# A chain of thirteen transformer stages on one core: first stage from x laid out by feature, gate rows ahead of a tile's turn, other banks in the forgetting attention

## The chip, the cores and the metric

The kernel runs on one core of a Trainium2 chip. The metric is the device time of one execution in microseconds; a lower one is better. Times are medians over several executions on the same chip. The core has a matrix engine (TensorE, PE in the profile), a vector engine (VectorE, DVE), an activation engine (ScalarE, ACT), a general engine (GpSimd, POOL) and a queue engine (SyncE, SP). Each runs its own list of instructions in order; semaphores hold one engine until another has come to a point.

## The reference

There are 256 tokens of 1024 features in float32. Two layers and a third block follow each other. Cut to what matters:

```python
x = x + 0.5 * swiglu(rmsnorm(x, g), w_in, w_out)        # stage 0, and four more like it
x = x + hgrn2_mixer(rmsnorm(x, g), ...)                 # layer 0
x = x + fox_mixer(rmsnorm(x, g), ...)                   # layer 1: forgetting attention, 16 heads of 64
h = h + 0.5 * gate * rms_norm(swiglu_2(u, ...), post)   # u = rms_norm(h, pre) * (1 + scale) + shift
h = h + gate * rms_norm(token_mixer(u, ...), post)      # third block: shift, scale and gate come from c
h = h + 0.5 * gate * rms_norm(swiglu_2(u, ...), post)

def rmsnorm(x, g): return x * rsqrt(mean(x * x) + 1e-6) * g
def swiglu(h, w_in, w_out): gate, up = split(h @ w_in); return (silu(gate) * up) @ w_out   # width 2816
```

## The kernel before

Every product is done in three parts: an operand is split into a rounded half (`w_hi`, `actT_hi`) and the rest (`w_lo`, `actT_lo`), and TensorE adds hi x hi, hi x lo and lo x hi into one bank of PSUM. SyncE's queue loads weights into four slots of `raw` (a slot is 128 x 2048 numbers, four blocks of 128 features by 512 columns), ScalarE rounds a slot into `w_hi` (L1370), VectorE subtracts (L1928). The activations come as features by tokens: TensorE transposes the scaled rows `xn` (L611, `turn_tile`), ScalarE rounds them out of PSUM with the norm's weight as scale (L1389) and VectorE makes the rest (L1950).

A feed-forward stage works through 11 chunks of 256 hidden columns (512 with the gate's). The gate and up products of a chunk fill bank 4 (tile 0) and bank 5 (tile 1), each tile of 128 tokens takes 24 products. ScalarE applies silu to the gate's half of a bank, first tile 0 (L1519, waits for `up0_done`), then tile 1 (L1523), and VectorE multiplies by the up half (L2095). Only then may `up(c + 1, 0)` write the same bank. In chunks 1 to 10 the down products of the chunk before lie in between; between chunk 0 and chunk 1 there is nothing.

The first chunk of a stage is `rounded_first`: tile 0's 16 products with `actT_hi` (L654), then its 8 with `actT_lo` (L662) with `between()` in their middle, then tile 1's. `between()` transposes tile 1, and in the third block's feed-forward stages (norm 6 and norm 8) also writes a row of gates across the partitions with 8 transposes (L835, `gate_wide_row`), which nothing needs until the stage's end.

The stage at the start: SyncE loads tile 0 of x, eight quarter-slot pieces of weights (256 KB each; slot 0, then slot 1), tile 1 of x, and two pieces of slot 3. ScalarE's queue loads the identity matrix and the norm's weights as rows. TensorE runs five products of ones to start (L1332), turns the weights' rows into columns, then tile 0. Later vectors (72 columns of biases among them) are loaded as rows by eleven DMAs of GpSimd and turned by two transposes after chunk 4 (`turn_vectors`, L1342 and L1343).

In the forgetting attention TensorE writes the negative running sum of the log gates into bank 5 (L1007), VectorE copies and splits it (L2343 to L2350), and the turned queries and keys of the first half go to banks 6, 7, 4, 5 (L1019), those of the second half to banks 1, 2, 3, 7. Keys are copied out of the first two banks by VectorE (L2356), queries out of the last two by ScalarE (L1687). Products of later column units, `unit(c, t)`, go to bank 0 for tile 0 and to bank 7 for tile 1.

## Time and profile before

| | us |
|---|---|
| median of 3 runs (lowest, highest) | 1580.67 (1580.09, 1581.17) |
| the profiled execution's own time | 1580.04 |
| its span in the trace | 1578.2 |
| TensorE busy | 1563.0 |
| VectorE busy | 1130.0 |
| ScalarE busy | 825.0 |

The trace covers one execution. The span runs from the first to the last instruction; 1.84 us of the profiled time lie around it. A row of the timeline is one instruction or several alike (x4), with its start and duration in us; brackets at its end tell how long its engine had been idle and what ended that.

### The profile page before, as it was taken

How to read it: one execution, taken by the hardware profiler on the slowest of the kernel's cores; microseconds unless marked ns; L12 is line 12 of the kernel's file. 1: busy time of each engine (PE TensorE's matmuls, PEld its weight loads, DVE VectorE, ACT ScalarE, POOL GpSimd, SP SyncE). 2: the span in 40 equal slices, each digit the busy share in tenths (PEclk: the TensorE clock that was granted, in tenths of full speed). 3: DMA queues.
4: the chain of work that ended last, by engine and by line, in shares of the span. 5: the costliest groups of instructions: out<-in, count | busy, mean ns of one | idle time of the engine just before them, and what ended most of it. 6: DMA issues, size and time to landing. Idle time of an engine off the chain costs nothing.

```text
span 1578.2 us, 22308 instructions
## 1 busy us (share of the span) xinstructions
PE 1563.0 (99%) x8273; PEld 1294.6 (82%) x8273; DVE 1130.0 (72%) x1271; ACT 825.0 (52%) x1007; POOL 67.1 (4%) x101
## 2 busy tenths in 40 slices
PE   8999999999999999999999999999999999999998
PEld 6888888888888888887888888888887988878886
DVE  6565668868776877776867877787787567775654
ACT  6465564654445544465655444554447666574443
POOL 2000100000000000000000000000000000000000
PEclk9999999999999999999999999999999999999999
DMA  8766653359887688845345988668884444456662
GB/s 281 223 206 215 228 200 123 129 173 299 278 264 260 209 276 281 280 165 182 109 159 186 301 265 276 236 217 271 274 306 153 171 161 149 145 173 214 210 208 87
DMA packets 242385, 337.09 MB, mean 214 GB/s; under 512 B 14217, under 2 KB 180322, under 8 KB 242320
## 3 DMA queue, kind: packets, MB, share of 16 engines
q1 hardware_dynamic: 196320, 281.05, 53.9%
q0 software_dynamic: 11232, 39.33, 6.8%
q10 hardware_dynamic: 34768, 15.83, 4.0%
q8 instruction: 42, 0.69, 0.2%
q14 instruction: 23, 0.19, 0.0%
HBM read 319.38 MB, written 1.05 MB: 203 GB/s over the span
## 4 chain that ended last, share of the span: by engine, by line
PE 94%; DVE 3%; ACT 2%; DMA 1%; issue 0%; SPq 0%; DVEq 0%; ACTq 0%
PE ps L602 28%; PE ps L604 28%; PE ps L603 28%; PE ps L654 3%; PE ps L662 2%; PE ps L611 1%; DVE w_lo L1928 1%; ACT w_hi L1370 1%; DMA raw<-ffn_w_in_dram 1%; DVE arena L1963 0%; PE ps L877 0%; PE ps L1037 0%; PE ps L1063 0%; PE ps L1187 0%; ACT arena L1418 0%
## 5 line engine op out<-in xcount | busy, mean ns | idle before, releaser
L1928 DVE TENSOR_TENSOR w_lo<-raw,w_hi 128x2048 fp32r<-128x2048 f32 x264 | 601.7, 2288 | 198.0 <-ACT w_hi L1370 196.9
L1370 ACT CAST w_hi<-raw 128x2048 fp32r<-128x2048 f32 x264 | 502.1, 1911 | 322.1 <-PE ps L604 290.1
L602 PE MATMUL ps<-w_hi,actT_hi 128*128 128x512 f32 x1392 | 546.5, 393 | 1.1 <-ACT arena L1687 0.7
L604 PE MATMUL ps<-w_hi,actT_lo 128*128 128x512 f32 x1392 | 542.1, 389 | 0.0
L603 PE MATMUL ps<-w_lo,actT_hi 128*128 128x512 f32 x1392 | 541.8, 389 | 0.0
L602 PEld LDWEIGHTS ps<-w_hi,actT_hi 128*128 128x128 f32 x1392 | 261.3, 188 | 57.9 <-issue 3.3
L604 PEld LDWEIGHTS ps<-w_hi,actT_lo 128*128 128x128 f32 x1392 | 261.3, 188 | 54.6
L603 PEld LDWEIGHTS ps<-w_lo,actT_hi 128*128 128x128 f32 x1392 | 261.4, 188 | 53.3
L602 PE MATMUL ps<-w_hi,hT_hi 128*128 128x512 f32 x480 | 187.4, 390 | 0.0
L604 PE MATMUL ps<-w_hi,hT_lo 128*128 128x512 f32 x480 | 186.9, 389 | 0.0
L603 PE MATMUL ps<-w_lo,hT_hi 128*128 128x512 f32 x480 | 186.8, 389 | 0.0
L2095 DVE TENSOR_TENSOR hidden<-gate,ps 128x256 f32<-128x256 f32 x132 | 77.9, 595 | 84.8 <-ACT gate L1523 76.2
L602 PEld LDWEIGHTS ps<-w_hi,hT_hi 128*128 128x128 f32 x480 | 90.1, 188 | 18.8
L603 PEld LDWEIGHTS ps<-w_lo,hT_hi 128*128 128x128 f32 x480 | 90.1, 188 | 18.7
L604 PEld LDWEIGHTS ps<-w_hi,hT_lo 128*128 128x128 f32 x480 | 90.1, 188 | 18.7
L1523 ACT ACTIVATE gate<-ps 128x256 f32<-128x256 f32 x66 | 25.4, 384 | 143.8 <-PE ps L604 124.1
L2113 DVE SCALAR_TENSOR_TENSOR arena<-arena,c_silu 128x512 f32<-128x512 f32 x126 | 94.3, 748 | 2.5
L593 POOL DMA_DIRECT2D arena<-w_ada_dram x72 | 51.3, 712 | 924.2 <-DVE arena L2113 634.2
L654 PE MATMUL ps<-w_hi,actT_hi 128*128 128x512 f32 x144 | 57.3, 398 | 3.5 <-ACT actT_hi L1389 2.9
L654 PE MATMUL ps<-w_lo,actT_hi 128*128 128x512 f32 x144 | 56.2, 391 | 0.0
L1519 ACT ACTIVATE gate<-ps 128x256 f32<-128x256 f32 x66 | 25.3, 384 | 54.3 <-PE ps L604 54.2
L2080 DVE STREAM_TRANSPOSE arena<-hidden 128x512 f32<-128x512 f32 x60 | 42.7, 712 | 3.8
(304 smaller groups left out, 1301.3 us busy)
## 6 DMA issues: line engine op xcount, KB each, us to landing
raw<-ffn_w_in_dram SPq DMA_DIRECT2D x172, 512.0 KB, 4.9
raw<-ffn_w_out_dram SPq DMA_DIRECT2D x88, 512.0 KB, 4.6
arena<-w_ada_dram POOLq DMA_DIRECT2D x72, 512.0 KB, 5.3
raw<-ffn_w_gate_dram SPq DMA_DIRECT2D x44, 512.0 KB, 4.0
raw<-ffn_w_up_dram SPq DMA_DIRECT2D x44, 512.0 KB, 5.0
raw<-ffn_w_down_dram SPq DMA_DIRECT2D x44, 512.0 KB, 4.4
raw<-w_in_dram SPq DMA_DIRECT2D x40, 512.0 KB, 4.5
raw<-hg_w_in_dram SPq DMA_DIRECT2D x32, 512.0 KB, 4.7
```

Of the source, the lines that this page charges most:

```text
L593: nc.gpsimd.dma_start(ada_raw[:, n % 2, :, :], w_ada[:, ks:ks + ADA_KS, j * ADA_FOLD:(j + 1) * ADA_FOLD])\
L602: nc.tensor.matmul(to, hi, whi, start=start, stop=False, skip_group_check=True)
L603: nc.tensor.matmul(to, hi, wlo, start=False, stop=False, skip_group_check=True)
L604: return nc.tensor.matmul(to, lo, whi, start=False, stop=stop, skip_group_check=True)
L654: nc.tensor.matmul(to, actT_hi[:, k, tok], half[:, s, w], start=k == 0 and half is w_hi, stop=False, skip_group_check=True)
L662: last = nc.tensor.matmul(to, actT_lo[:, k, tok], w_hi[:, s, w], start=False, stop=k == KD - 1, skip_group_check=True)
L1370: nc.scalar.copy(w_hi[:, s, :], raw[:, s, :]).then_inc(hi_ready[s], 1)
L1523: nc.scalar.activation(gate[:, 1, :], ps[:, UP_BANK + 1, 0:FC], ACT.Silu).then_inc(gate_ready, 1)
L1928: nc.vector.tensor_tensor(w_lo[:, s, :], raw[:, s, :], w_hi[:, s, :].bitcast(F32), ALU.subtract)\
L2080: nc.vector.transpose(hid_blocks.rearrange("p b n -> p (b n)"), hidden.rearrange("p t f -> p (t f)"))\
L2095: nc.vector.tensor_tensor(to, g, u, ALU.mult).then_inc(hidden_ready, 1)
L2113: total = nc.vector.scalar_tensor_tensor(acc_j, part, c_silu[:, k:k + 1], acc_j, ALU.mult, ALU.add)
```

## The change

It has four parts.

1. Stage 0 reads a second copy of x that is already features by tokens (`x_turned`, prepared with the other inputs). ScalarE rounds it with the norm's weight as scale, VectorE makes the rest, without the token's factor 1/rms. GpSimd squares x and adds the eight feature blocks into one, TensorE sums over the partitions with two products of one column, and the factor is applied behind the products: as the scale of the silu and as a factor in the product with the up half. TensorE no longer transposes anything in stage 0. Its first chunk is `loaded_chunk`, in which both tiles go side by side, in parts of four products, in the order in which the halves of the slots and their rests come. x itself is loaded later, for the residual.
2. All small vectors come as one table of columns (`columns`), so `turn_vectors` and eleven loads fall away.
3. In `between()` the row of gates comes ahead of tile 1's transposes.
4. In the forgetting attention the running sum goes to bank 3 in place of bank 5, and VectorE's copy of it is waited for within `chunk(1, 1)`, ahead of its second tile; the second half's keys and queries go to banks 7, 1, 2, 3.

```diff
+                        if half == 0:
+                            nc.sync.dma_start(x_turned[:, 4:8, :], a["x_turned"][:, 4:8, :]).then_inc(x_turned_loaded, 16)
...
-            load_x(0)
+                nc.sync.dma_start(x[:, t, :], a["x"][0, t * P:(t + 1) * P, :]).then_inc(x_loaded, 16)
...
                     up_weights(st, 2)
+                    if st.norm == 0:
+                        load_x(0)
+                        load_x(1)
...
+            pool.wait_ge(head_loaded, 32)
+            step.mark(nc.gpsimd.tensor_tensor(x_squares[:, 0:4, :], x_turned[:, 0:4, :], x_turned[:, 0:4, :], ALU.mult))
+            pool.wait_ge(x_turned_loaded, 16)
+            step(nc.gpsimd.tensor_tensor(x_squares[:, 4:8, :], x_turned[:, 4:8, :], x_turned[:, 4:8, :], ALU.mult))
+            for n in (4, 2):
+                step(nc.gpsimd.tensor_tensor(x_squares[:, 0:n, :], x_squares[:, 0:n, :], x_squares[:, n:2 * n, :], ALU.add))
+            nc.gpsimd.tensor_tensor(x_squares[:, 0, :], x_squares[:, 0, :], x_squares[:, 1, :], ALU.add).then_inc(squares, 2)
             pool.wait_ge(actT_ready, 4)
-            at = 48
...
             nc.gpsimd.dma_start(fox_b, a["fox_b_f"]).then_inc(small_loaded, 16)
...
-            nc.gpsimd.dma_start(consts[:, P:], a["consts"][:, P:]).then_inc(consts_loaded, 16)
+            nc.gpsimd.dma_start(consts[:, :], a["consts"]).then_inc(consts_loaded, 16)
...
                 def between():
-                    turn_tile(st, xn, 1)
                     if st.kind == "ffn" and st.norm >= 6:
                         gate_wide_row(st.norm - 6)
+                    turn_tile(st, xn, 1)
                 rounded_first(st, banks[0], 0, between).then_inc(tile0_done, 1)
                 rounded_first(st, banks[1], 1)
...
+            def loaded_chunk(st):
+                def part(s, kks, act, weights, start=False, stop=False):
+                    for t in range(TILES):
+                        for kk in kks:
+                            k, w = 4 * s + kk, slice(kk * COLS, (kk + 1) * COLS)
+                            last = nc.tensor.matmul(ps[:, UP_BANK + t, :], act[:, k, t * P:(t + 1) * P], weights[:, s, w],
+                                                    start=start and kk == 0, stop=stop and kk == 3, skip_group_check=True)
+                        if stop and t == 0:
+                            last.then_inc(up0_done, 1)
+                    return last
...
+                def sums():
+                    pe.wait_ge(squares, 2)
+                    for t in range(TILES):
+                        last = nc.tensor.matmul(ps[:, SMALL_BANK, t:t + 1], x_squares[:, 0, t * P:(t + 1) * P], hidden[:, 0, 0:1],
+                                                start=True, stop=True, skip_group_check=True)
+                    last.then_inc(first_sum, 1)
+                for s in range(2):
+                    pe.wait_ge(actT_hi_ready, s + 1)
+                    pe.wait_ge(front_hi, s + 1)
+                    part(s, (0, 1), actT_hi, w_hi, start=s == 0)
+                    if s == 0:
+                        pe.wait_ge(front_lo, 1)
+                        part(s, (0, 1), actT_hi, w_lo)
+                    pe.wait_ge(actT_ready, s + 1)
+                    part(s, (0, 1), actT_lo, w_hi)
+                    if s:
+                        pe.wait_ge(front_lo, 2)
+                        part(s, (0, 1), actT_hi, w_lo)
+                        sums()
+                    pe.wait_ge(hi_ready[s], 1)
+                    part(s, (2, 3), actT_hi, w_hi)
+                    part(s, (2, 3), actT_lo, w_hi)
+                    pe.wait_ge(lo_ready[s], 1)
+                    part(s, (2, 3), actT_hi, w_lo, stop=s == 1).then_inc(split_used[s], 1)
...
-                first_chunk(st, [ps[:, UP_BANK + t, :] for t in range(TILES)], up0_done)
+                if st.norm:
+                    first_chunk(st, [ps[:, UP_BANK + t, :] for t in range(TILES)], up0_done)
+                else:
+                    loaded_chunk(st)
...
+                with pe.Fori(2, NF - 1) as c:
+                    middle(c)
                 if st.norm == 0:
-                    with pe.Fori(2, VECTORS_AT) as c:
-                        middle(c)
-                    turn_vectors()
-                    with pe.Fori(VECTORS_AT, NF - 1) as c:
-                        middle(c)
-                else:
-                    with pe.Fori(2, NF - 1) as c:
-                        middle(c)
+                    pe.wait_ge(consts_loaded, 32)
...
+                        if t and s % 2 == 0 and second_tile is not None:
+                            second_tile()
...
-                    nc.tensor.matmul(ps[:, 5, 0:T], C["neg_spread"][0:FOX_H, :], fx_cT, start=True, stop=True)                        .then_inc(fx_spread, 1)
+                    pe.wait_ge(kept1, st.kept + 2)
+                    nc.tensor.matmul(ps[:, 3, 0:T], C["neg_spread"][0:FOX_H, :], fx_cT, start=True, stop=True)                        .then_inc(fx_spread, 1)
...
-                        if bank == 5:
-                            pe.wait_ge(fx_negc_ready, 3)
...
-                chunk(st, 1, 1)
+                chunk(st, 1, 1, lambda: pe.wait_ge(fx_negc_ready, 3))
...
-                turn(1, (1, 2, 3, 7))
+                turn(1, (7, 1, 2, 3))
                 weigh(0)
-                pe.wait_ge(fx_qT_ready, 4)
+                pe.wait_ge(fx_kT_ready, 3)
...
-            pe.wait_ge(head_loaded, 32)
-            nc.tensor.transpose(ps[:, SMALL_BANK, 0:48], rows_a[0:48, :], ident[0:48, 0:48]).then_inc(cols_turned, 1)
-            warm(1)
...
-                if st.norm == 0:
-                    turn_tile(st, xn, 0)
...
+            def first_stage(st):
+                def front(s):
+                    act.wait_ge(front_loaded[s], 32)
+                    nc.scalar.copy(w_hi[:, s, 0:SLOT // 2], raw[:, s, 0:SLOT // 2]).then_inc(front_hi, 1)
+                def back(s):
+                    act.wait_ge(raw_loaded[s], 32)
+                    nc.scalar.copy(w_hi[:, s, SLOT // 2:SLOT], raw[:, s, SLOT // 2:SLOT]).then_inc(hi_ready[s], 1)
+                def rounded(s):
+                    for k in range(4 * s, 4 * s + 4):
+                        last = nc.scalar.activation(actT_hi[:, k, :], x_turned[:, k, :], ACT.Copy, scale=norm_cols[:, k:k + 1])
+                    last.then_inc(actT_hi_ready, 3 if s else 1)
+                front(0)
+                act.wait_ge(head_loaded, 32)
+                rounded(0)
+                back(0)
+                act.wait_ge(x_turned_loaded, 16)
+                rounded(1)
+                front(1)
+                back(1)
+                split_hi(3, st.filled[3])
+                act.wait_ge(first_sum, 1)
+                nc.scalar.activation(n_std[:, 0:2], ps[:, SMALL_BANK, 0:2], ACT.Sqrt, bias=eps_col, scale=1.0 / D).then_inc(stds, 2)
...
+                    scale = [first_rstd[:, t:t + 1] if st.norm == 0 else 1.0 for t in range(TILES)]
+                    if st.norm == 0:
+                        act.wait_ge(first_scale, 1)
                     act.wait_ge(up0_done, n + c + 1)
-                    nc.scalar.activation(gate[:, 0, :], ps[:, UP_BANK, 0:FC], ACT.Silu).then_inc(gate_ready, 1)
+                    nc.scalar.activation(gate[:, 0, :], ps[:, UP_BANK, 0:FC], ACT.Silu, scale=scale[0]).then_inc(gate_ready, 1)
...
-                queries(1, (3, 7))
+                queries(1, (2, 3))
...
-            nc.scalar.dma_start(ident, a["consts"][:, 0:P]).then_inc(head_loaded, 16)
-            nc.scalar.dma_start(rows_a[0:48, :], a["norm_g"].rearrange("l i (k p) -> (l i k) p", p=P)).then_inc(head_loaded, 16)
+            nc.scalar.dma_start(x_turned[:, 0:4, :], a["x_turned"][:, 0:4, :]).then_inc(head_loaded, 16)
+            nc.scalar.dma_start(cols[:, 0:COLUMNS], a["columns"]).then_inc(head_loaded, 16)
             act.wait_ge(memsets_done, 2)
             load_sqrt()
-            after_out(None, stages[0])
+            first_stage(stages[0])
...
+            def first_stage(st):
+                def rest(s, part):
+                    at = slice(part * SLOT // 2, (part + 1) * SLOT // 2)
+                    if part:
...
+                        dve.wait_ge(front_hi, s + 1)
                     nc.vector.tensor_tensor(w_lo[:, s, at], raw[:, s, at], w_hi[:, s, at].bitcast(F32), ALU.subtract)\
-                        .then_inc(lo, 1)
+                        .then_inc(lo_ready[s] if part else front_lo, 1)
...
+                def unrounded(s):
+                    dve.wait_ge(actT_hi_ready, s + 1)
+                    for k in range(4 * s, 4 * s + 4):
+                        last = nc.vector.scalar_tensor_tensor(actT_lo[:, k, :], x_turned[:, k, :], norm_cols[:, k:k + 1],
+                                                              actT_hi[:, k, :].bitcast(F32), ALU.mult, ALU.subtract)
+                    last.then_inc(actT_ready, 3 if s else 1)
+                rest(0, 0)
+                dve.wait_ge(head_loaded, 32)
+                unrounded(0)
+                rest(0, 1)
+                dve.wait_ge(x_turned_loaded, 16)
+                unrounded(1)
+                rest(1, 0)
+                rest(1, 1)
+                split_lo(3, st.filled[3])
+                dve.wait_ge(stds, 2)
+                nc.vector.reciprocal(first_rstd, n_std[:, 0:2]).then_inc(first_scale, 1)
...
+                    if st.norm == 0 and t == 0:
+                        dve.wait_ge(x_loaded, 32)
...
@@ -2092,7 +2151,10 @@
                         to, g, u = hidden[:, t, :], gate[:, t, :], ps[:, UP_BANK + t, FC:COLS]
                         if turn:
                             to, g, u = hidden_block(t), by_block(g), by_block(u)
-                        nc.vector.tensor_tensor(to, g, u, ALU.mult).then_inc(hidden_ready, 1)
+                        if st.norm == 0:
+                            nc.vector.scalar_tensor_tensor(to, u, first_rstd[:, t:t + 1], g, ALU.mult, ALU.mult).then_inc(hidden_ready, 1)
+                        else:
+                            nc.vector.tensor_tensor(to, g, u, ALU.mult).then_inc(hidden_ready, 1)
...
-                keys(1, (1, 2))
+                keys(1, (7, 1))
...
-    arrays = {name: np.ascontiguousarray(inputs[name]) for name in INPUTS}
+    arrays = {name: np.ascontiguousarray(inputs[name]) for name in INPUTS if name not in COLUMN_INPUTS}
+    arrays["columns"] = columns(inputs)
+    arrays["x_turned"] = np.ascontiguousarray(np.asarray(inputs["x"])[0].T.reshape(KD, P, T).transpose(1, 0, 2))
```

How the instructions stand, at the three places that the prediction speaks of. First ScalarE at the program's start; before, from the rounding of slot 3 to the first silu (`gate` is the silu's output, `ps` is PSUM):

```order
L1370 CAST w_hi<-raw 128x2048 [waits raw_loaded3]
L1389 ACTIVATE actT_hi<-ps,cols 128x128 [waits turned]
L1389 ACTIVATE actT_hi<-ps,cols 128x128 x3
L1389 ACTIVATE actT_hi<-ps,cols 128x128 [waits turned]
L1389 ACTIVATE actT_hi<-ps,cols 128x128 x3
L1519 ACT_TABLE_LOAD
L1519 ACTIVATE gate<-ps 128x256 [waits up0_done]
L1523 ACTIVATE gate<-ps 128x256 [waits split_used1]
```

And with the change, from the first rounding of x on:

```order
L1493 ACTIVATE actT_hi<-arena,cols 128x256 [waits head_loaded]
L1493 ACTIVATE actT_hi<-arena,cols 128x256 x3
L1489 CAST w_hi<-raw 128x1024 [waits raw_loaded0]
L1493 ACTIVATE actT_hi<-arena,cols 128x256 [waits x_turned_loaded]
L1493 ACTIVATE actT_hi<-arena,cols 128x256 x3
L1485 CAST w_hi<-raw 128x1024 [waits front_loaded1]
L1489 CAST w_hi<-raw 128x1024 [waits raw_loaded1]
L1387 CAST w_hi<-raw 128x2048 [waits raw_loaded3]
L1506 ACTIVATE small<-ps,small 128x2 [waits first_sum]
L1553 ACT_TABLE_LOAD [waits up0_done]
L1553 ACTIVATE gate<-ps,small 128x256 [waits first_scale]
L1557 ACTIVATE gate<-ps,small 128x256 [waits split_used1]
```

The table load stood ahead of any wait and now stands behind the wait for `up0_done`; the silu itself waits for `first_scale`. Next TensorE at the end of the first chunk (`arena` holds the squares, `hidden` the ones). Before, the last rows of tile 1 and the first of chunk 1:

```order
L654 MATMUL ps<-w_lo,actT_hi 128x512
L654 MATMUL ps<-w_hi,actT_hi 128x512
L654 MATMUL ps<-w_lo,actT_hi 128x512
L662 MATMUL ps<-w_hi,actT_lo 128x512 [waits actT_ready]
L662 MATMUL ps<-w_hi,actT_lo 128x512 x3
L662 MATMUL ps<-w_hi,actT_lo 128x512 [waits actT_ready]
L662 MATMUL ps<-w_hi,actT_lo 128x512 x3
L602 MATMUL ps<-w_hi,actT_hi 128x512 [waits hidden_ready,lo_ready3]
L603 MATMUL ps<-w_lo,actT_hi 128x512
L604 MATMUL ps<-w_hi,actT_lo 128x512
```

With the change:

```order
L675 MATMUL ps<-w_hi,actT_lo 128x512 [waits actT_ready]
L675 MATMUL ps<-w_hi,actT_lo 128x512 x3
L675 MATMUL ps<-w_lo,actT_hi 128x512 [waits front_lo]
L675 MATMUL ps<-w_lo,actT_hi 128x512 x3
L684 MATMUL ps<-hidden,arena 128x1 [waits squares]
L684 MATMUL ps<-hidden,arena 128x1
L675 MATMUL ps<-w_hi,actT_hi 128x512 [waits hi_ready1]
L675 MATMUL ps<-w_hi,actT_hi 128x512 x3
L675 MATMUL ps<-w_hi,actT_lo 128x512 x4
L675 MATMUL ps<-w_lo,actT_hi 128x512 [waits lo_ready1]
L675 MATMUL ps<-w_lo,actT_hi 128x512 x3
L598 MATMUL ps<-w_hi,actT_hi 128x512 [waits hidden_ready,lo_ready3]
```

Tile 0's last product stood 25 products ahead of chunk 1; now it stands among the last four. Last, TensorE in the forgetting attention, before, from the running sum to the next chunk of weights:

```order
L1007 MATMUL ps<-arena,consts_sb 128x256 [waits fx_c]
L1019 MATMUL ps<-consts_sb,arena 128x128 [waits fx_normed]
L1019 MATMUL ps<-consts_sb,arena 128x128 x11
L1019 MATMUL ps<-consts_sb,arena 128x128 [waits fx_negc_ready]
L1019 MATMUL ps<-consts_sb,arena 128x128 x3
L602 MATMUL ps<-w_hi,actT_hi 128x512 [waits lo_ready2,kept1,kept0]
L603 MATMUL ps<-w_lo,actT_hi 128x512
```

With the change:

```order
L1037 MATMUL ps<-arena,consts_sb 128x256 [waits kept1,fx_c]
L1047 MATMUL ps<-consts_sb,arena 128x128 [waits fx_normed]
L1047 MATMUL ps<-consts_sb,arena 128x128 x15
L598 MATMUL ps<-w_hi,actT_hi 128x512 [waits lo_ready2,kept1,kept0]
L599 MATMUL ps<-w_lo,actT_hi 128x512
```

The wait for the split running sum (`fx_negc_ready`) is gone from between the transposes; it now stands twelve products further on.

## Rows read from the trace of the kernel before

**Rows 1.** The page's first lines: span, and busy time of each engine.

```profile
span 1578.2 us, 22308 instructions
...
PE 1563.0 (99%) x8273; PEld 1294.6 (82%) x8273; DVE 1130.0 (72%) x1271; ACT 825.0 (52%) x1007; POOL 67.1 (4%) x101
```

**Rows 2.** Waits of TensorE over the span: us in total, times, longest.

```profile
PE ps L654 <- ACT actT_hi L1389: 2.9, 3, 1.9
```

**Rows 3.** Timeline, 5 to 16 us: start, us, engine, line, operation, [idle before].

```profile
5.86 0.70 PE L1332 MATMUL ps<-hidden 128*128 128x256 f32 x2
...
6.49 1.05 ACT L1470 CAST w_hi<-raw 128x1024 fp32r<-128x1024 f32 x1
...
7.57 1.23 DVE L1935 TENSOR_TENSOR w_lo<-raw,w_hi 128x1024 fp32r<-128x1024 f32 x1
8.00 1.04 ACT L1472 CAST w_hi<-raw 128x1024 fp32r<-128x1024 f32 x1 [0.47 <-DMA raw<-ffn_w_in_dram]
8.95 1.14 ACT L1389 ACTIVATE actT_hi<-ps,cols 128x128 fp32r<-128x128 f32 x4
...
10.14 0.50 PE L654 MATMUL ps<-w_hi,actT_hi 128*128 128x512 f32 x1 [1.86 <-ACT actT_hi L1389]
10.22 1.12 DVE L1950 SCALAR_TENSOR_TENSOR actT_lo<-ps,cols,actT_hi 128x128 fp32r<-128x128 f32 x4
...
15.20 1.91 ACT L1370 CAST w_hi<-raw 128x2048 fp32r<-128x2048 f32 x1 [0.76 <-DMA raw<-ffn_w_in_dram]
```

**Rows 4.** Timeline, 19 to 25 us: the first activations and products behind chunk 0.

```profile
19.20 1.28 ACT L1519 ACT_TABLE_LOAD   x1
...
20.49 0.39 ACT L1519 ACTIVATE gate<-ps 128x256 f32<-128x256 f32 x1
...
23.77 0.39 PE L602 MATMUL ps<-w_hi,actT_hi 128*128 128x512 f32 x1
...
23.97 0.38 ACT L1523 ACTIVATE gate<-ps 128x256 f32<-128x256 f32 x1 [3.09 <-PE ps L662]
...
24.00 0.39 PE L603 MATMUL ps<-w_lo,actT_hi 128*128 128x512 f32 x1
...
24.39 0.62 DVE L2095 TENSOR_TENSOR hidden<-gate,ps 128x256 f32<-128x256 f32 x1 [2.37 <-ACT gate L1523]
```

**Rows 5.** GpSimd's groups of instructions: busy us, mean ns, idle before.

```profile
L580 POOL CAST hidden<-arena 128x112 uint8<-128x112 f32 x1 | 2.4, 2396 | 153.4 <-PE ps L711 153.4
L582 POOL MEMSET arena<- 128x2048 f32 x1 | 1.8, 1811 | 0.1
```

**Rows 6.** Windows of TensorE at the end: busy us (count), granted clock, DMA.

```profile
1574.00:1578.20 4.20, 0.00 (x0) 0.72 0.33 125
```

**Rows 7.** Timeline of TensorE at 89 us, around the turned vectors.

```profile
88.83 0.39 PE L604 MATMUL ps<-w_hi,hT_lo 128*128 128x512 f32 x1
89.06 0.26 PE L1342 MATMUL ps<-consts_sb,arena 116*128 116x116 f32 x1
...
89.50 0.40 PE L603 MATMUL ps<-w_lo,actT_hi 128*128 128x512 f32 x1
```

**Rows 8.** Timeline in the forgetting attention, at 734 us.

```profile
733.90 0.66 PE L1019 MATMUL ps<-consts_sb,arena 128*128 128x128 f32 x4 [0.47 <-DVE hT_lo L2350]
```

**Rows 9.** Timeline in the forgetting attention, at 771 us.

```profile
771.42 0.50 PE L602 MATMUL ps<-w_hi,actT_hi 128*128 128x512 f32 x1 [0.74 <-ACT arena L1687]
```

**Rows 10.** Timeline of the last feed-forward stage's start.

```profile
1394.42 1.09 PE L611 MATMUL ps<-consts_sb,arena 128*128 128x128 f32 x8 [1.22 <-DVE arena L1974]
...
1395.36 1.04 PE L835 MATMUL ps<-consts_sb,mod_gate 128*128 128x128 f32 x8
...
1399.69 1.36 DVE L1963 TENSOR_SCALAR arena<-ps,mod_scale,modc 128x128 f32<-128x128 f32 x4
...
1401.08 0.69 DVE L1966 TENSOR_TENSOR actT_lo<-arena,actT_hi 128x512 fp32r<-128x512 f32 x1
```

**Rows 11.** Timeline of the stage before the mixer, at 1032 us.

```profile
1031.72 0.50 PE L662 MATMUL ps<-w_hi,actT_lo 128*128 128x512 f32 x1 [0.50 <-DVE actT_lo L1966]
```

97 lines of the change are left out of this document (31 added, 66 removed).

## Prediction

> **What bounds the kernel now.** I read the page's first lines first: TensorE is busy for 1563.0 of the span's 1578.2 us [rows 1], so only about 15 us are not already its own work, and whatever the other engines save is worth nothing unless TensorE waited for it. So next come TensorE's waits: the largest group is 2.9 us in three waits for the rounding of x (L1389) at the start, the longest 1.9 [rows 2]. Then I read the timeline at each place that the change touches. At the start TensorE gets its first real product at 10.14 us, after 1.86 idle [rows 3], and the first product of chunk 1 at 23.77 [rows 4]. Products follow each other every 0.23 us (23.77 to 24.00 [rows 4]), although a row shows 0.39 for one, because they overlap. In the forgetting attention there are two waits, 0.47 us for the split running sum [rows 8] and 0.74 us for ScalarE's copy of the queries [rows 9]. In the third block TensorE waits 1.22 us ahead of tile 1's transposes [rows 10] and 0.50 us at the end of another first chunk [rows 11].
>
> **Part 1, the start.** Two times decide: when the first product can start and when chunk 1 can start.
>
> Loads: slot 0 had landed at 8.00 and slot 3 at 15.20 (both casts waited for their DMA [rows 3]). Between them 2.5 MB came, so 2.88 us per MB. Ahead of 8.00 stood x's tile (0.5 MB), some 0.09 MB of small things and slot 0 (1 MB). Now `x_turned`'s first half, the columns and slot 0 stand there, the same sum. So slot 0's front half is there 0.5 MB earlier, at 6.5, `x_turned`'s second half at 8.0 + 1.4 = 9.4, slot 1 by 12.3 and slot 3 as before at 15.2.
>
> ScalarE: the front half takes 1.05 [rows 3], 6.5 to 7.55. Then four roundings of 128x256: four of 128x128 took 1.14; the slope of the casts (1.91 for 2048 columns, 1.05 for 1024 [rows 3]) adds 0.11 to each, so 1.6, to 9.15. First product at 9.2 in place of 10.14. Further: back half to 10.2, second roundings to 11.8, slot 1 to 13.9, slot 3 from 15.2 to 17.1, all of it early (below).
>
> VectorE: 1.23 for the front's rest (7.6 to 8.8), then four rests of x: 1.12 for 128x128 [rows 3], and about 0.13 more each, 1.65, so 9.2 to 10.85. TensorE wants them after eight products, at 11.0. I name this cover because it is the thinnest: 0.15 us. The later halves end at 12.1, 13.75, 15.0 and 16.2, and TensorE wants them after 20, 28, 32 and 44 products, at 13.8, 15.6, 16.6 and 19.6.
>
> So TensorE runs 48 products without a gap, 11.0 us, and two products of one column, for which I take 0.3 (two transposes cost 0.2, below): 9.2 to 20.5. That is 3.3 us ahead of 23.77. Most of it is not kept. Chunk 1 writes the same bank and waits for tile 0's hidden values. Before, tile 0 was complete 25 products earlier, and ScalarE loaded silu's table at 19.20 and was through at 20.9 [rows 4], long ahead of TensorE. Now tile 0's last product starts 0.7 ahead of the end and is complete at about 20.2. And the order of instructions shows the table load behind the wait for `up0_done`. So from 20.2: 1.28 table load, 0.39 silu, 0.62 product of VectorE [rows 4], and 0.1 for three hand-overs (VectorE started 0.04 behind its silu): 22.6. Gain of part 1: 23.77 - 22.6 = 1.1 us, with a new idle stretch of TensorE of about 2.1 us. What is queued behind it is all of TensorE's work; VectorE's hidden value of tile 1 follows in 0.6, ahead of tile 0's twelve products.
>
> Of the table load the row shows 1.28 and the silu 0.01 behind it [rows 4]. The Trainium skill (ScalarE: Activation LUTs, What ACT_TABLE_LOAD costs) adds a drain of about 1.38 to each switch of sets; by that the new idle stretch would be 3.5 and the kernel 1579.5. The row does not show such a drain, so I leave it out.
>
> The same move of the load is in the loop that runs after the small vectors, five passes. There tile 1's silu waits for twelve more products, 2.8 us, and 1.28 + 0.39 lie within these. Cost nothing; without that cover up to 5 x 1.28 = 6.4 us.
>
> Squares: GpSimd has four of its five operations, 2816 columns, behind the landing at 9.4. No row shows such an operation. A memset of 2048 columns takes 1.81 [rows 5]: 2.5 us for 2816, done at 11.9. A cast of 112 columns takes 2.40 [rows 5]: if that is a fixed price of an instruction, 4 x 2.4 + 2.5 = 12.1, done at 21.5. TensorE asks after 36 products, at 17.5. A product of two inputs moves about three times what a memset does, which gives 7.4 us and 16.8; I take that, no wait, and keep 4.0 us as the upper end. The skill (GPSIMD Engine Reference, Elementwise — side-by-side cycle accounting) has 4.5 us for 2048 columns of an addition; that would be done at 15.6, and the sum stays.
>
> Vectors: `turn_vectors` stretched 88.83 to 89.50 by 0.67 where two products take 0.46 [rows 7]: gain 0.2. The eleven loads that fall away ran beside the products. x's two loads move behind chunk 2's weights; the residual wants them at the stage's end, some 170 us on. Slot 1's second filling is asked for when VectorE is done with the first, 16.2; 1 MB at 2.88 and some 2 us on the way land near 21.5, and ScalarE turns to it at 22. It is wanted after chunk 1's first half, 5.5 us later than 22.6, so a late landing has 1 to 2 us of cover.
>
> **Part 3, gate rows first.** The eight transposes take 0.9 us (1394.42 to 1395.36 for their like) and would fit into the wait of 1.22 [rows 10]. But the chunk's end is VectorE's: its last block starts at 1399.69, takes 1.36, and the rest another 0.69 from 1401.08 [rows 10], done at 1401.8. TensorE arrived there at 1395.36 + 0.9 + 24 x 0.23 = 1401.8 before. So arriving 0.6 to 0.9 earlier only makes a wait there: gain 0. In the other stage the transposes of tile 1 come 0.9 later, ScalarE's rounding with them, and the wait of 0.50 for VectorE at 1031.72 [rows 11] takes that up: cost 0. Together I keep +0.9 and -0.4 as ends.
>
> **Part 4, banks.** The wait of 0.47 [rows 8] goes: `fx_negc_ready` is now wanted twelve products (2.8 us) later and came at 733.9. TensorE's new wait on bank 3 is for a copy that `chunk(1, 1)` waited for anyway. The wait of 0.74 [rows 9] goes too: bank 7 is turned first and read by VectorE, which is idle there, and ScalarE's copies come behind its exponentials as before, but nobody waits for them. Gain 0.5 + 0.7 = 1.2. No TensorE row shows a wait between there and the end of that stage that it could reappear in. Ends: 0.6 and 1.2.
>
> **Sum.** 1.1 + 0.2 + 0 + 1.2 = 2.5 us. Against the profiled execution's 1580.04 that is 1577.5; the median of the runs is 0.6 above that execution, so 1578.2. A measurement of this kernel can tell about 0.2% (3.2 us) from no change; 2.5 us is 0.16%.
>
> **Rivals.**
> - *More comes back*: the load of the table is not paid behind `up0_done`, the head lands earlier than 6.5, or gate rows pay 0.9. With 1.3 for the first: 3.8 us, 1576.9. For it: my times at the start use bounds that were waits on other things. Against: the order of the instructions is plain.
> - *Squares late*: GpSimd needs more than 8.1 us from 9.4. Up to the fixed price it is 4.0 us lost, 1582.2; from 13.8 us on (5.7 lost) the kernel is slower by more than 0.2%. Nothing else covers it, since TensorE's last twelve products stand behind the two small ones.
> - *Slower by the clock*: the products of ones end near 6.6 [rows 3] and TensorE then idles 2.6 us in place of 1.86. In the last 4.2 us of the trace, where TensorE does nothing, the granted clock is 0.72 [rows 6], so it does fall from 2.4 to 1.2 GHz in idleness. At the lower level a product takes 0.23 us more; 25 such products (5.7 us) make it slower by over 0.2%, all 48 give 1578.2 + 11 = 1589. Against: the waits of 1.86 and less did not let it fall.
> - *The start does nothing*: `x_turned` lands 1.4 us late on the shared queues and part 1 is worth 0: 1579.3.
>
> **Chances.** Forecast 0.55 (1577.3 to 1579.0, of which 0.05 falls under 1577.5), more 0.22, squares late 0.14 (0.10 within 0.2%, 0.04 beyond), clock 0.04, start does nothing 0.05. So faster 0.27, same 0.65, slower 0.08. The range reaches down to 1576.4 (the forecast with table load and gate rows less a little) and up to 1580.9 (a wait of 2.7 us for the squares).
>
> **What would show it.** Right: first product near 9.2; a table load of ScalarE right behind tile 0's last product; chunk 1 from about 22.6; no wait at the two places of the forgetting attention; a longer wait for VectorE's rest at the end of the last stage's first chunk. Wrong: a wait of TensorE for GpSimd ahead of the one-column products, a granted clock under 1 in the first 20 us, products spaced over 0.23, or a TensorE wait in the last stage that is gone without another in its place.

## The result and the profile after

The changed kernel takes 1587.68 us (median of 6 runs, 1585.78 to 1588.15), the kernel before 1580.92 in the same comparison. The ratio is 1.0043 with a 95% interval of 1.0031 to 1.0054: 6.8 us slower. The forecast was 1578.2 (1576.4 to 1580.9), and slower by over 0.2% had a chance of 0.08.

The profiled execution took 1587.27 us with a span of 1585.5, so 7.3 more than before's 1578.2 [rows 1]. The page's first lines:

```profile
span 1585.5 us, 22260 instructions
...
PE 1566.1 (99%) x8258; PEld 1296.7 (82%) x8258; DVE 1133.1 (71%) x1255; ACT 822.3 (52%) x994; POOL 68.6 (4%) x95
```

TensorE is busy 3.1 us longer, although it has 15 products fewer: a first hint that some ran slower. The rest is waiting. Its three longest waits (us in total, times, longest), all of the first stage:

```profile
PE ps L675 <- DVE actT_lo L1979: 3.7, 1, 3.7
PE ps L675 <- ACT actT_hi L1493: 3.2, 1, 3.2
PE ps L598 <- DVE hidden L2155: 2.2, 1, 2.2
```

The third was forecast (2.1), the second nearly (2.6). The first, on VectorE's `actT_lo` of L1979, the rests of x, was not. The timeline around it (start, us, then the idle time ahead in brackets), to be held against [rows 3]:

```profile
7.08 1.04 ACT L1485 CAST w_hi<-raw 128x1024 fp32r<-128x1024 f32 x1 [3.82 <-DMA raw<-ffn_w_in_dram]
...
8.16 1.75 DVE L1973 TENSOR_TENSOR w_lo<-raw,w_hi 128x1024 fp32r<-128x1024 f32 x1 [8.16 <-ACT w_hi L1485]
...
9.79 1.62 PE L675 MATMUL ps<-w_hi,actT_hi 128*128 128x512 f32 x4 [3.19 <-ACT actT_hi L1493]
...
9.85 6.90 DVE L1979 SCALAR_TENSOR_TENSOR actT_lo<-arena,cols,actT_hi 128x256 fp32r<-128x256 f32 x4
...
16.81 1.77 PE L675 MATMUL ps<-w_hi,actT_lo 128*128 128x512 f32 x4 [3.69 <-DVE actT_lo L1979]
17.81 1.66 DVE L1979 SCALAR_TENSOR_TENSOR actT_lo<-arena,cols,actT_hi 128x256 fp32r<-128x256 f32 x4
```

The first cast starts at 7.08, when its DMA has landed (6.5 in the forecast), and the first product at 9.79, 0.35 ahead of before's 10.14. Behind its eighth product TensorE waits 3.69 us, because four rests of x take 6.90 us. The same four instructions on the other half of x, from 17.81, take 1.66. The only difference that the trace shows is what GpSimd does meanwhile. In narrow stretches of the timeline of GpSimd and then of VectorE the instructions of that stretch stand one by one:

```profile
9.80 1.89 POOL L561 TENSOR_TENSOR arena<-arena 128x1024 f32<-128x1024 f32 x1 [0.97 <-DMA arena<-x_turned_dram]
...
11.77 2.43 POOL L563 TENSOR_TENSOR arena<-arena 128x1024 f32<-128x1024 f32 x1
...
14.27 1.33 POOL L563 TENSOR_TENSOR arena<-arena 128x512 f32<-128x512 f32 x1
...
15.75 0.72 POOL L564 TENSOR_TENSOR arena<-arena 128x256 f32<-128x256 f32 x1
...
9.85 2.12 DVE L1979 SCALAR_TENSOR_TENSOR actT_lo<-arena,cols,actT_hi 128x256 fp32r<-128x256 f32 x1
...
11.89 2.59 DVE L1979 SCALAR_TENSOR_TENSOR actT_lo<-arena,cols,actT_hi 128x256 fp32r<-128x256 f32 x1
...
14.40 1.48 DVE L1979 SCALAR_TENSOR_TENSOR actT_lo<-arena,cols,actT_hi 128x256 fp32r<-128x256 f32 x1
...
15.81 0.95 DVE L1979 SCALAR_TENSOR_TENSOR actT_lo<-arena,cols,actT_hi 128x256 fp32r<-128x256 f32 x1
```

Add start and duration. GpSimd's operations end at 11.69, 14.20, 15.60 and 16.47; VectorE's rests end at 11.97, 14.48, 15.88 and 16.76. Each rest ends 0.28 or 0.29 us behind one operation of GpSimd: VectorE gets one instruction through for each of GpSimd's, however long that is. The row at 8.16 fits in: a rest of weights takes 1.75 there (1.23 before [rows 3]) beside GpSimd's first square, which runs from 6.94 to 8.83.

The second loss is the clock. TensorE's windows (from and to, us, busy, count, granted clock as a share of full speed, then DMA's share and GB/s):

```profile
10.00:15.00 5.00, 3.12 (x8) 0.66 0.99 312
15.00:20.00 5.00, 3.19 (x8) 0.72 0.00 1
...
25.00:30.00 5.00, 3.29 (x17) 1.00 1.04 369
30.00:35.00 5.00, 4.46 (x13) 0.66 1.05 348
```

Before, the same windows all show 1.00. Now the granted clock fell from 2.4 to 1.2 GHz just behind the idle stretch of 3.19 us, just behind the one of 3.69, and again just behind the 2.25 ahead of chunk 1 (narrower windows show it at half from about 10.4, 17.2 and 30.8). Behind that last one nine products take from 30.54 to 34.25, 3.71 us in place of 2.07.

How chunk 1 comes to start at 30.54 (before 23.77 [rows 4]):

```profile
27.92 1.28 ACT L1553 ACT_TABLE_LOAD   x1 [2.15 <-PE ps L675]
29.22 0.47 ACT L1553 ACTIVATE gate<-ps,small 128x256 f32<-128x256 f32 x1
...
30.54 0.50 PE L598 MATMUL ps<-w_hi,actT_hi 128*128 128x512 f32 x1 [2.25 <-DVE hidden L2155]
```

The table load stands behind `up0_done`, as forecast, and the silu follows it at once.

The other parts went nearly as forecast. Neither wait of [rows 8, 9] has a like in the changed kernel. New is an idle stretch of 0.59 us of TensorE at 266.51, in layer 0, for which the trace shows no cause ("issue"). In the last stage, to be held against [rows 10]:

```profile
1401.68 1.10 PE L607 MATMUL ps<-consts_sb,arena 128*128 128x128 f32 x8 [0.35 <-DVE arena L2031]
...
1408.35 0.69 DVE L2023 TENSOR_TENSOR actT_lo<-arena,actT_hi 128x512 fp32r<-128x512 f32 x1
```

The wait ahead of tile 1's transposes is 0.35 in place of 1.22, and VectorE's last rest stands where it stood: from 1408.35, 7.27 behind before's 1401.08 [rows 10]. The stage's first product is as late, 1395.76 against 1388.51, so the stage gained nothing.

### The profile page after: what moved, and what is told of

The parts are those of the page before. It is cut to its first block, busy times and chain, and to the rows that moved or that the text cites. A ratio compares the mean times of both kernels' runs of the same rounds, so it can differ in the third digit from the quotient of the medians.

```text
span 1585.5 us, 22260 instructions
## 1 busy us (share of the span) xinstructions
PE 1566.1 (99%) x8258; PEld 1296.7 (82%) x8258; DVE 1133.1 (71%) x1255; ACT 822.3 (52%) x994; POOL 68.6 (4%) x95
## 3 DMA queue, kind: packets, MB, share of 16 engines
HBM read 320.43 MB, written 1.05 MB: 203 GB/s over the span
## 4 chain that ended last, share of the span: by engine, by line
PE 94%; DVE 3%; ACT 1%; issue 1%; DMA 0%; DVEq 0%; SPq 0%; ACTq 0%
PE ps L598 28%; PE ps L600 28%; PE ps L599 28%; PE ps L645 3%; PE ps L653 1%; PE ps L607 1%; DVE w_lo L1962 1%; PE ps L675 1%; DVE arena L2020 1%; PE ps L906 0%; PE ps L1065 0%; PE ps L1108 0%; DMA raw<-ffn_w_in_dram 0%; PE ps L1091 0%; PE ps L1215 0%
## 5 line engine op out<-in xcount | busy, mean ns | idle before, releaser
L2157 DVE TENSOR_TENSOR hidden<-gate,ps 128x256 f32<-128x256 f32 x110 | 64.1, 591 | 65.3 <-ACT gate L1557 58.0
L1557 ACT ACTIVATE gate<-ps 128x256 f32<-128x256 f32 x55 | 21.1, 384 | 115.3 <-PE ps L600 99.6
L1545 ACT CAST hT_hi<-arena 128x512 fp32r<-128x512 f32 x60 | 36.9, 616 | 27.7 <-DMA arena<-arena 27.7
L2144 DVE TENSOR_TENSOR hT_lo<-arena,hT_hi 128x512 fp32r<-128x512 f32 x60 | 41.1, 686 | 9.6 <-ACT hT_hi L1545 9.6
```

The lines of the kernel that those rows point to most:

```text
L1545: nc.scalar.copy(hT_hi.rearrange("p f t -> p (f t)").rearrange("p (n a j) -> p n a j", n=4, a=4), hT_columns)\
L1557: nc.scalar.activation(gate[:, 1, :], ps[:, UP_BANK + 1, 0:FC], ACT.Silu, scale=scale[1]).then_inc(gate_ready, 1)
L2144: nc.vector.tensor_tensor(hT_lo.rearrange("p f t -> p (f t)").rearrange("p (n a j) -> p n a j", n=4, a=4), hT_columns, hT_hi.bitcast(F32). ...
L2157: nc.vector.tensor_tensor(to, g, u, ALU.mult).then_inc(hidden_ready, 1)
```

## The experiments

The main theory is that GpSimd's squares hold VectorE's rests of x, and that the waits of TensorE that this makes also pull its clock down. Each expectation names its rivals. "Ratio" is always to the kernel before, with its 95% interval.

**The changed kernel without GpSimd's operations.** The factor 1/rms is made from ones, so this version leaves out the norm's scale.

```diff
-            step.mark(nc.gpsimd.tensor_tensor(x_squares[:, 0:4, :], x_turned[:, 0:4, :], x_turned[:, 0:4, :], ALU.mult))
...
+            nc.gpsimd.memset(small[:, 24:25], 0.0).then_inc(squares, 2)
```

> The changed kernel without GpSimd's five operations: the factor 1/rms is made from ones in place of the squares of x, so stage 0 is not scaled rightly. Theory A (GpSimd's two-input operations hold VectorE up): VectorE's four rests of x from 9.9 us take 1.7 us in place of 6.90, TensorE's wait of 3.7 us behind its eighth product is gone, and with it the second stretch at the lower clock; the first stretch stays, since TensorE still idles 3.2 us ahead of its first product. Time 1581.5 to 1583. Rival B (the rests are slow because of their own form, two inputs from SBUF and a column as scalar, or because they are the first of their kind): 6.9 us stays and the time stays at 1587.

1581.76 us, ratio 1.0007 (0.9998 to 1.0016): 5.7 us of the 6.8 lost are gone (0.0036 of 1581). Its timeline:

```profile
10.08 2.07 PE L669 MATMUL ps<-w_hi,actT_hi 128*128 128x512 f32 x4 [4.21 <-ACT actT_hi L1487]
10.15 1.67 DVE L1973 SCALAR_TENSOR_TENSOR actT_lo<-arena,cols,actT_hi 128x256 fp32r<-128x256 f32 x4 [0.47 <-ACT actT_hi L1487]
...
26.39 0.47 PE L592 MATMUL ps<-w_hi,actT_hi 128*128 128x512 f32 x1 [2.25 <-DVE hidden L2149]
```

Four rests take 1.67 us and no wait for them is left. The clock was still low here from about 8.4 to 15.2 (it fell in the 4.21 us of idle ahead of the first product), so the low clock at the start alone is not what cost most. The profile is the slowest of this version's ten runs (1583.34 us), with an idle stretch like that of layer 0 above, here 1.1 us.

**The same operations put into the kernel before**: six products of two inputs on a spare region, nothing else changed.

```diff
+            for n in (1024, 1024, 1024, 1024, 512, 256):
+                step(nc.gpsimd.tensor_tensor(spare[0][:, 0:n], spare[0][:, 0:n], spare[1][:, 0:n], ALU.mult))
```

> The kernel before with six two-input operations of GpSimd from 5.4 us on (4 x 1024, 512 and 256 columns of a spare region that nothing reads), about 9 us of them. Theory A (GpSimd holds VectorE up): VectorE's subtractions of 1024 columns take 1.7 us or more in place of 1.23 while GpSimd works, its scaling of x and rests of x too, TensorE's first product comes 1 to 4 us later, 1583 to 1588. Rival B: VectorE's durations stay and the time is 1580.9.

1587.47 us, ratio 1.0043 (1.0028 to 1.0059). Nobody waits for these results, and yet they cost 6.8 us. GpSimd's and then VectorE's timeline:

```profile
5.31 14.53 POOL L562 TENSOR_TENSOR arena<-arena 128x1024 f32<-128x1024 f32 x6 [2.45 <-DMA arena<-norm_g_dram]
...
6.49 3.95 DVE L1981 TENSOR_SCALAR arena<-x,small 128x512 f32<-128x512 f32 x2
10.35 6.68 DVE L1942 TENSOR_TENSOR w_lo<-raw,w_hi 128x1024 fp32r<-128x1024 f32 x2
16.96 1.11 DVE L1957 SCALAR_TENSOR_TENSOR actT_lo<-ps,cols,actT_hi 128x128 fp32r<-128x128 f32 x4
```

The like in VectorE's timeline of before:

```profile
6.65 0.88 DVE L1974 TENSOR_SCALAR arena<-x,small 128x512 f32<-128x512 f32 x2
...
11.26 2.35 DVE L1935 TENSOR_TENSOR w_lo<-raw,w_hi 128x1024 fp32r<-128x1024 f32 x2
```

The operation with one input in SBUF (TENSOR_SCALAR) takes 3.95 in place of 0.88; two weights' rests with both inputs in SBUF take 6.68 in place of 2.35; four rests with one input in PSUM take 1.11, as before (1.12 [rows 3]), while GpSimd still runs. So it is not GpSimd's activity as such but access to SBUF. The 6.8 us are again hold and clock together: the granted clock is at half from about 10 to 23.6.

**Only writes in that place**: eight memsets of GpSimd in the kernel before.

```diff
+            for n in range(8):
+                step(nc.gpsimd.memset(spare, 1.0))
```

> The kernel before with eight memsets of GpSimd over 128x2048 of a spare region (1.81 us each by its own row, about 14.6 us, from 5.3 to 20), where the earlier run had six two-input operations in the same stretch. They only write. Theory A (what holds VectorE is GpSimd's reading of two inputs beside VectorE's second input): the weights' rests stay at 1.23 each and the four-fold rests at 1.12, and the time is 1581 within 0.15%; at most the operation with one input in SBUF (the TENSOR_SCALAR of 128x512) is held, for one or two memsets, 2 to 3 us, 1583 to 1584. Theory B (any GpSimd instruction in that stretch holds VectorE): as with the two-input operations, 1587.

1582.25 us, ratio 1.0013 (1.0003 to 1.0022).

```profile
5.46 15.50 POOL L559 MEMSET arena<- 128x2048 f32 x8 [4.37 <-DMA arena<-norm_g_dram]
...
6.62 2.95 DVE L1978 TENSOR_SCALAR arena<-x,small 128x512 f32<-128x512 f32 x2
9.49 2.34 DVE L1939 TENSOR_TENSOR w_lo<-raw,w_hi 128x1024 fp32r<-128x1024 f32 x2
11.75 1.11 DVE L1954 SCALAR_TENSOR_TENSOR actT_lo<-ps,cols,actT_hi 128x128 fp32r<-128x128 f32 x4
```

GpSimd is busy as long, but two weights' rests take 2.34, undisturbed. Only the TENSOR_SCALAR is held (2.95 for 0.88). The first real product comes 0.7 later for it (10.84), and the clock is at half from about 8.3 to 15; how the 1.9 us divide between the two was not separated. So an instruction of VectorE with two SBUF inputs is held by GpSimd's reading, not by its writing. The Trainium skill (SBUF — State Buffer, Who interferes with whom) states this: VectorE's second input comes through a read port that it shares with GpSimd, the shared pair is an exclusive lock held for a whole instruction, and an operation of one input in a two-port mode takes the pair as well. The first two agree with the rows (6.68 beside reads, 2.34 beside writes; each rest ends behind one whole instruction of GpSimd). That TENSOR_SCALAR is held by either (3.95 and 2.95) fits the third, but no run shows the mode that it ran in.

**Squares in pieces** of 256 columns, 15 instructions in place of five.

```diff
-            step(nc.gpsimd.tensor_tensor(x_squares[:, 4:8, :], x_turned[:, 4:8, :], x_turned[:, 4:8, :], ALU.mult))
+                step(nc.gpsimd.tensor_tensor(x_squares[:, k:k + 1, :], x_turned[:, k:k + 1, :], x_turned[:, k:k + 1, :], ALU.mult))
```

> The changed kernel with GpSimd's squares and sums cut to one block of 256 columns each: 15 instructions in place of five, the same elements. In the changed kernel's timeline the four rests of x end 0.28 us behind the end of one GpSimd instruction each (rest 1 at 11.97 behind 11.69, rest 2 at 14.48 behind 14.20). Theory A (the two engines take turns by whole instructions, so that VectorE gets one instruction through for each one of GpSimd's): a turn is then about 0.5 + 0.3 us, the rests take 3.0 to 3.5 us in place of 6.90, from 9.85 to about 13; TensorE's wait for them falls from 3.7 to about 1; GpSimd ends later, near 17.5, and a wait of up to 1 us for the sum is possible. Time 1583 to 1585. Theory B (the engines share a bandwidth, VectorE is slowed by the elements that GpSimd moves): the rests stay at 6 to 7 us and the time at 1587.

```profile
7.15 6.02 POOL L563 TENSOR_TENSOR arena<-arena 128x256 f32<-128x256 f32 x7
...
9.95 2.75 DVE L1983 SCALAR_TENSOR_TENSOR actT_lo<-arena,cols,actT_hi 128x256 fp32r<-128x256 f32 x4 [0.43 <-ACT actT_hi L1497]
...
21.76 0.61 PE L688 MATMUL ps<-hidden,arena 128*128 128x1 f32 x4 [1.06 <-POOL arena L568]
```

The same elements, and the rests take 2.75 in place of 6.90: turns by instruction, not a shared bandwidth. But the time is 1587.64 us, ratio 1.0051 (1.0034 to 1.0068), no gain: of the expectation the durations came true and the time did not. Each of GpSimd's pieces now waits for VectorE in its turn, the sums end late, TensorE waits 1.06 us for them at 21.76, and VectorE's second four rests and two weights' rests take 3.60 and 3.43 us. Its runs scatter from 1584.56 to 1589.84; the profile is the fastest of them (span 1582.8), so what the slower ones lost is not in a trace.

**Squares behind the first rests**: GpSimd's second square waits until they are made.

```diff
+            pool.wait_ge(actT_ready, 1)
```

> The changed kernel, but GpSimd's second square waits until VectorE has made the first four rests of x. Theory A: the first rests take 1.7 us and end at 11.5, TensorE's first wait for them is gone (or 0.5), but the remaining four GpSimd instructions, 11.5 to about 18.5, now take turns with the weights' rest and the second four rests, which end at 18 to 19 where TensorE asks at 16.3: a wait of 2 to 3 us there, and the sums end about 18.5. So the stall moves rather than goes: 1584.5 to 1587. Theory B (only the first rests matter, because they alone had thin cover): 1582 to 1583, as without GpSimd's squares.

1584.69 us, ratio 1.0025 (1.0016 to 1.0035), 2.8 us better by the ratios.

```profile
10.02 1.67 DVE L1980 SCALAR_TENSOR_TENSOR actT_lo<-arena,cols,actT_hi 128x256 fp32r<-128x256 f32 x4 [0.47 <-ACT actT_hi L1494]
...
12.74 6.96 DVE L1980 SCALAR_TENSOR_TENSOR actT_lo<-arena,cols,actT_hi 128x256 fp32r<-128x256 f32 x4
...
19.75 1.20 PE L676 MATMUL ps<-w_hi,actT_lo 128*128 128x512 f32 x4 [1.10 <-DVE actT_lo L1980]
```

The first four rests take 1.67 and the second four now 6.96: the hold moved to work with more cover, and of it 1.10 us reach TensorE.

**More products of ones** ahead of the first product.

```diff
-WARM = 6
+WARM = 13
```

> The changed kernel with 13 products of ones alone; GpSimd's operations stay. Theory A (two causes that add up): the first stretch at the lower clock goes, VectorE's rests still take some 6.5 us, TensorE waits some 5 us for them and the clock falls in that wait and stays low for some 3.5 us behind it. Chunk 1 some 1 to 2 us earlier than in the changed kernel, 1585.5 to 1586.5. Rival B (the clock is the larger cause): 1583 or less.

1587.17 us, ratio 1.0038 (1.0025 to 1.0051): not to be told from the changed kernel, where theory A had expected 1 to 2 us less.

```profile
5.00:10.00 5.00, 5.00 (x19) 1.00 1.05 374
...
15.00:20.00 5.00, 3.65 (x9) 0.50 0.00 1
```

The clock stays full through the first eight products and then falls in the wait for the rests, now 4.44 us. As long as that wait is there, TensorE only arrives at it earlier. Without GpSimd's operations the same edit is worth something (both edits together):

```diff
-WARM = 6
+WARM = 13
...
+            nc.gpsimd.memset(small[:, 24:25], 0.0).then_inc(squares, 2)
```

> The changed kernel without GpSimd's five operations (the factor is made from ones, as in e1) and with 13 products of ones in place of 6, so that TensorE is busy until its first real product. Theory A (the clock falls because TensorE idles some 4 us there): granted clock 1.00 through the first chunk, its 48 products in 11 us, chunk 1 at 23.3 us, in place of 26.4 in e1: 1578.7. Rival B (the clock falls for another cause, or the ones push the first product back by what they save): 1581 to 1582.

1580.14 us, ratio 0.9994 (0.9985 to 1.0004), some 2 us less than without them and with 6 ones. Timeline of TensorE, and then one of its windows:

```profile
23.90 0.47 PE L592 MATMUL ps<-w_hi,actT_hi 128*128 128x512 f32 x1 [2.24 <-DVE hidden L2149]
```

```profile
25.00:30.00 5.00, 5.00 (x18) 0.72 1.07 354
```

Chunk 1 starts at 23.90 (26.39 with 6 ones, after the same wait), but the clock falls behind the wait of 2.24. The profile is the slowest of ten runs here too (1581.39 us). Up to chunk 1 it has neither hold nor low clock, and yet chunk 1 starts 0.13 behind before's 23.77: the new start by itself gained nothing.

**Silu's table ahead of the wait for tile 0**: the first silu's two waits are swapped.

```diff
+                    act.wait_ge(up0_done, n + c + 1)
                     if st.norm == 0:
                         act.wait_ge(first_scale, 1)
-                    act.wait_ge(up0_done, n + c + 1)
```

> The changed kernel with the two waits of the first silu in the other order, so that the table load stands behind the wait for the scale and ahead of the wait for the finished bank. Theory A (the table load behind the finished bank costs its 1.28 us, and the idleness it makes longer lets the clock fall): TensorE's wait ahead of chunk 1 is 1.0 in place of 2.25 us, the granted clock stays 1.00 behind it, so 1.3 + 1.7 = 3 us less, 1584.5. Rival B: only the 1.3 us, and the clock falls all the same: 1586.2.

1585.6 us, ratio 1.0033 (1.0021 to 1.0045): 1.6 us better by the ratios.

```profile
26.82 1.28 ACT L1553 ACT_TABLE_LOAD   x1 [0.28 <-DVE small L1993]
...
29.98 0.47 PE L598 MATMUL ps<-w_hi,actT_hi 128*128 128x512 f32 x1 [0.91 <-DVE hidden L2155]
```

The load now stands behind the scale, the wait that is written last, and runs under tile 0's products; the wait ahead of chunk 1 is 0.91, and the clock behind it stays at 1.00. That is theory A's mechanism, but half of its 3 us: in this trace the clock is at half from about 8.7 to 22.3, longer than in the changed kernel, and chunk 1 starts only 0.56 earlier.

**All three removed**: no squares, 13 ones, swapped waits.

```diff
-WARM = 6
+WARM = 13
...
+            nc.gpsimd.memset(small[:, 24:25], 0.0).then_inc(squares, 2)
...
+                    act.wait_ge(up0_done, n + c + 1)
                     if st.norm == 0:
                         act.wait_ge(first_scale, 1)
-                    act.wait_ge(up0_done, n + c + 1)
```

> e5 with the two waits of the first silu swapped as in e2 (the factor again made from ones): what the new first stage would be worth if its three costs were gone. Theory A: TensorE's wait ahead of chunk 1 shrinks to some 1 us, chunk 1 at 22.1 us, 1577.3, and slower than the forecast's 22.6 by nothing: 0.2% faster than before. Rival B: no gain over e5, since VectorE's rest of slot 3 or tile 0's hidden values end the wait at the same time: 1578.7.

1577.79 us, ratio 0.9983 (0.9974 to 0.9992), 9.5 us better than the changed kernel by the ratios.

```profile
20.12 1.28 ACT L1547 ACT_TABLE_LOAD   x1 [1.13 <-DVE small L1987]
...
22.73 0.47 PE L592 MATMUL ps<-w_hi,actT_hi 128*128 128x512 f32 x1 [1.22 <-DVE hidden L2149]
```

The clock is 1.00 throughout the start. The load stands at 20.12, behind the reciprocal of the sums, and 1.22 us of idle remain.

**The squares on ScalarE** (a complete version): ScalarE squares x behind its last head cast, VectorE adds twice, TensorE sums with four products of one column, tile 0's last six products come first, 13 ones, the swapped waits, and silu's table is loaded right behind the root.

```diff
+                for half in range(2):
+                    k = slice(4 * half, 4 * half + 4)
+                    step.mark(nc.scalar.activation(x_squares[:, k, :], x_turned[:, k, :], ACT.Square))
...
+                nc.scalar.activation(sqrt_col, eps_col, ACT.Silu)
```

> The changed kernel, complete, with the squares on ScalarE and their sums on VectorE and TensorE (two additions, four products of one column), tile 0's last six products ahead of tile 1's, silu's table loaded behind the root, and 13 products of ones. Theory A: VectorE's rests take 1.7 us, the granted clock stays 1.00, chunk 1 starts near 23 us, and parts 2 and 4 give their 1.4 us: 1577.8 to 1579, 0.1 to 0.2% faster than before. Rival B: VectorE's two additions (1.9 us) delay the rest of slot 3 and with it chunk 1, to 24 us or more: 1579.5 or more.

1578.86 us, ratio 0.9989 (0.9980 to 0.9998).

```profile
23.59 0.47 PE L591 MATMUL ps<-w_hi,actT_hi 128*128 128x512 f32 x1 [1.58 <-DVE hidden L2168]
```

Chunk 1 starts 0.2 ahead of before, the clock is 1.00 and nothing is held.

**Pieces, 13 ones and swapped waits together**, complete: the edits of three runs above in one kernel.

```diff
-WARM = 6
+WARM = 13
...
+                step(nc.gpsimd.tensor_tensor(x_squares[:, k:k + 1, :], x_turned[:, k:k + 1, :], x_turned[:, k:k + 1, :], ALU.mult))
```

> The changed kernel, complete, with three edits: GpSimd's squares and sums in pieces of one block, 13 products of ones in place of 6, and silu's table loaded ahead of the wait for tile 0. Theory A (turns by instruction, and clock and table as the earlier runs showed): rests end near 13, TensorE's waits at the start are each 1 us or less, the granted clock stays 1.00, chunk 1 starts at 23.5 to 25, and the time is 1578.5 to 1580.5. Theory B: as with 13 ones alone, less 2 us for the table: 1585.

1586.09 us, ratio 1.0038 (1.0023 to 1.0052). That is 5.6 us over the upper end that the theory gave.

```profile
15.00:20.00 5.00, 4.28 (x19) 1.00 0.01 2
20.00:25.00 5.00, 3.95 (x14) 0.70 0.47 133
```

```profile
28.66 0.56 PE L602 MATMUL ps<-w_hi,actT_hi 128*128 128x512 f32 x1 [0.49 <-DVE hidden L2159]
```

TensorE waits 0.75 us for the rests and 1.05 for the sums (at 21.90). Behind the latter the clock falls and stays at half up to chunk 1, which starts at 28.66 where 25 was the upper end. So the expected full clock is what failed. The profile is the fastest of the five runs (1583.48 us); what the slower ones lost besides is not in a trace.

**The other parts alone**: the kernel before with only the gate rows and the banks (the diff's parts 3 and 4).

```diff
-                    turn_tile(st, xn, 1)
                     if st.kind == "ffn" and st.norm >= 6:
                         gate_wide_row(st.norm - 6)
+                    turn_tile(st, xn, 1)
...
-                turn(1, (1, 2, 3, 7))
+                turn(1, (7, 1, 2, 3))
```

> The kernel before with parts 3 and 4 alone (gate rows first; other banks). Forecast: the waits of 0.47 and 0.74 us go, the gate rows give nothing because VectorE ends the chunk, so 1.2 us less, 1579.6. Rival: the gate rows give their 0.9 us too, 1578.8; or the waits come back elsewhere, 1580.8.

1578.84 us, ratio 0.9989 (0.9980 to 0.9998); the span is 1577.0 against 1578.2. The forecast for these was 1.2, and that the spans differ by just this is in part luck: chunk 1, at a start that was not changed, comes 0.57 later here. From TensorE's transposes at 302.25 (302.63 here) to the last stage's first product at 1388.51 (1387.32 here) the trace gains 1.6.

## Why the prediction was wrong

**The step that failed** is "VectorE: 1.23 for the front's rest (7.6 to 8.8), then four rests of x: 1.12 for 128x128 [rows 3], and about 0.13 more each, 1.65, so 9.2 to 10.85". Alone they take 1.66, so the duration was right; beside GpSimd's squares they took 6.90. The prediction named this cover as the thinnest, 0.15 us, and asked of the squares only when they end (16.8 forecast, 16.47 measured), never what they hold while they run. The rows of before could not show it: GpSimd had no operation that reads two inputs. The turns read above, applied to the forecast's own times (four GpSimd instructions, the last ending at 16.8), would give rests that end near 17 in place of 10.85; this is an estimate. The rule of the Trainium skill cited with the memsets (SBUF — State Buffer, Who interferes with whom) says the same, and I had not weighed it.

**What the 7.9 us between 22.6 and 30.54 are**: first product 0.6 late (9.79); wait for the rests 3.7; the wait ahead of chunk 1 0.15 longer; and the rest, 3.5, in the products, which took 20.75 - 3.69 - 2.25 = 14.8 us where 48 at 0.23 and the two small ones make 11.3. At full clock (no squares, 13 ones) they took 23.90 - 9.96 - 2.24 = 11.7, so 3.1 of the 3.5 are the low clock. Behind chunk 1's start it cost 1.6 more (3.71 - 2.07). So 6.77 and 1.6, 8.4 later than before. At the second stage's first transposes it is 8.2 (200.16 against 191.94), which leaves 0.2 for the vectors; at those at 302.25 it is 8.9 (311.12), behind the unexplained idle stretch of 0.59; at the last stage's first product it is 7.25, so banks and gate rows gave 1.6. That is the span's 7.3.

**The rival "slower by the clock"** had a chance of 0.04 and its mechanism came true, in 3.1 + 1.6 = 4.7 us. How much of that follows from the rests was not separated. Without the squares 5.7 us came back, the wait of 3.69 with them, but the products ahead of chunk 1 still took 26.39 - 10.08 - 2.25 = 14.1 us, 2.4 over the 11.7; with 13 ones the first stretch was at full clock, but the wait grew to 4.44, the clock fell in it, and nothing was gained. Its argument against, that waits of 1.86 did not let the clock fall, did not even hold for waits of that size: in the version with pieces, table and ones it fell behind one of 1.05.

**Part 1's gain of 1.1 was mis-sized too.** Without hold and low clock, and with the table load where the forecast had it, chunk 1 starts at 23.90 (no squares, 13 ones), not at 22.6: the first product is 0.76 late (9.96; the head landed at 7.26, not 6.5), the products take 0.4 more than 11.3, and the wait ahead of chunk 1 0.14 more.

**"Squares late" did not come**: GpSimd ended at 16.47, a second ahead of the 17.5 at which they were due in the forecast.

**Right were** the table load behind `up0_done` (silu 0.02 behind the load), the gate rows at nothing (the last stage's wait shrank, the chunk's end stayed VectorE's), the vectors' small gain as far as the trace shows it, and the banks, whose two waits are gone, though the trace gives some 1.6 us for them in place of 1.2. The Trainium skill (ScalarE: Activation LUTs, What ACT_TABLE_LOAD costs) adds a drain of about 1.38 us to a switch of tables; no row here shows it: the silu starts 0.02 behind the load, and in the version with ScalarE's squares the load (20.88) starts 0.02 behind the root.

**The first stage from turned x** gained in these runs only with three more edits: with squares left out, 13 ones and the table ahead, chunk 1 starts at 22.73, 1.04 ahead of before. That this is near the 1.1 of the forecast is luck, since the forecast had the table load behind tile 0. A complete version with ScalarE's squares gave 0.2 of it. With the squares on GpSimd no run here beat the kernel before.

**What stays open**: why the version in pieces scatters by 5 us, what the idle stretch in layer 0 is, how the clock's 4.7 us divide, and why the clock fell after 2.25 us of idle in one kernel and not in another (last section).
